# Expert weights through three landing places and on-chip moves, instead of straight into a ring of six buffers

## The reference, cut to what matters

```python
def block_step(out, inp):
    toks, gw, e = inp
    xb = t[toks]
    a = jnp.minimum(xb @ w_gate[e] + b_gate[e], SWIGLU_LIMIT)
    b = jnp.clip(xb @ w_up[e] + b_up[e], -SWIGLU_LIMIT, SWIGLU_LIMIT)
    hid = a * jax.nn.sigmoid(SWIGLU_ALPHA * a) * (b + 1)
    y = hid @ w_down[e] + b_down[e]
    return out.at[toks].add((y * gw[:, None]).astype(out.dtype)), None
```

## Time and profile before

| | us |
|---|---|
| median of 3 runs (1394.22 to 1398.82) | 1398.72 |
| span of the profiled execution, first to last instruction | 1396.9 |
| PE busy | 1252.0 |
| DVE busy | 402.7 |
| POOL busy | 121.0 |

### The profile page before, as it was taken

One profiled execution on the slowest core, in us unless ns is written; L12 is line 12 of the kernel. 1 busy time (PEld: TensorE's weight loads), 2 busy tenths in 40 slices (PEclk: granted clock), 3 DMA queues, 4 the chain that ended last, 5 costly groups with the idle time before them and its releaser, 6 DMA issues.

```text
span 1396.9 us, 24933 instructions
## 1 busy us (share of the span) xinstructions
PE 1252.0 (90%) x10197; PEld 555.7 (40%) x10198; DVE 402.7 (29%) x896; ACT 260.1 (19%) x501; POOL 121.0 (9%) x168
## 2 busy tenths in 40 slices
PE   5999898568989999988999889988989999999996
PEld 2445445466654333333333333333333333333432
DVE  1265469817855121111111111111111112111112
ACT  2421432336041111111111111100000101100102
POOL 0211540185000000000000000000000000000000
PEclk9999999769988999999999999999999999999998
DMA  9958010010476999999999999999999699969994
GB/s 354 397 182 316 31 61 30 5 34 31 180 308 254 426 426 428 427 428 427 426 426 426 426 428 427 427 427 425 426 426 420 268 427 426 426 266 426 428 427 179
DMA packets 48135, 458.59 MB, mean 328 GB/s; under 512 B 4417, under 2 KB 4817, under 8 KB 22737
## 3 DMA queue, kind: packets, MB, share of 16 engines
q1 hardware_dynamic: 48080, 457.81, 79.1%
HBM read 456.15 MB, written 1.05 MB: 327 GB/s over the span
## 4 chain that ended last, share of the span: by engine, by line
PE 54%; DMA 34%; DVE 7%; issue 2%; ACT 1%; POOL 1%; DVEq 0%; SPq 0%; POOLq 0%; ACTq 0%
DMA arena<-in_w_up 33%; PE bank L1163 21%; PE bank L1190 8%; PE bank L673 7%; PE bank L1055 2%; PE bank L1124 2%; PE bank L584 2%; PE bank L544 1%; DVE arena L1737 1%; PE bank L1172 1%; DVE arena L2266 1%; DVE arena L2263 1%; DVE arena L2261 1%; DMA arena<-in_x 1%; PE bank L904 1%
## 5 line engine op out<-in xcount | busy, mean ns | idle before, releaser
L1163 PE MATMUL bank<-arena 128*64 128x512 f32 x2176 | 484.6, 595 | 43.7 <-DMA arena<-in_w_up 22.5
L1163 PEld LDWEIGHTS bank<-arena 128*64 128x64 f32 x2176 | 150.1, 136 | 359.3 <-issue 263.9
L1190 PE MATMUL bank<-arena 128*64 128x512 f32 x1088 | 239.2, 592 | 0.0
L2259 DVE TENSOR_SCALAR arena<-bank 128x512 f32<-128x512 f32 x34 | 23.6, 693 | 403.3 <-PE bank L1163 403.3
L1190 PEld LDWEIGHTS bank<-arena 128*64 128x64 f32 x1088 | 75.9, 136 | 140.5 <-issue 138.0
L673 PE MATMUL bank<-arena 128*128 128x512 f32 (+1 forms) x320 | 123.7, 540 | 0.0
L673 PEld LDWEIGHTS bank<-arena 128*128 128x128 f32 x320 | 60.7, 195 | 58.2 <-issue 55.3
L2190 DVE TENSOR_SCALAR arena<-arena 96x64 bf16<-96x64 f32 x35 | 8.8, 251 | 224.6 <-PE bank L1190 224.6
L1133 PE MATMUL bank<-arena 64*128 64x512 f32 x280 | 69.6, 614 | 0.8 <-ACT arena L1552 0.8
L1124 PE MATMUL bank<-arena 128*128 128x64 bf16 x1680 | 62.8, 198 | 1.1 <-DVE arena L2186 1.1
L1124 PEld LDWEIGHTS bank<-arena 128*128 128x128 bf16 x1680 | 62.9, 118 | 1.2 <-DVE arena L2186 1.2
(11 more groups left out here) (352 smaller groups left out, 1029.2 us busy)
## 6 DMA issues: line engine op xcount, KB each, us to landing
arena<-in_w_gate SPq DMA_DIRECT2D x64, 2048.0 KB, 22.5
arena<-in_w_up SPq DMA_DIRECT2D x64, 2048.0 KB, 24.1
arena<-in_w_down SPq DMA_DIRECT2D x64, 2048.0 KB, 22.0
arena<-in_w_ada SPq DMA_DIRECT2D x12, 2048.0 KB, 9.7
arena<-in_wfm SPq DMA_DIRECT2D x20, 512.0 KB, 3.4
arena<-in_wz SPq DMA_DIRECT2D x4, 1024.0 KB, 14.3
arena<-in_w_out SPq DMA_DIRECT2D x2, 2048.0 KB, 8.3
arena<-in_x SPq DMA_DIRECT2D x2, 1024.0 KB, 7.6
```

Source lines behind the costliest of these rows:

```text
L1163: last = mm(ps[m][64 * c_:64 * c_ + 64, :], xcT[:, k, :], ring[:, 2 * h_ + m, k % 4, 512 * c_:512 * c_ + 512], start=False, stop=(k == KT ...
L1190: last = mm(ps[2][64 * c_:64 * c_ + 64, :], hidT[:, k % 4, 64 * (k // 4):64 * (k // 4) + 64], ring[:, 4 + h_, k % 4, 512 * c_:512 * c_ + 5 ...
L2259: v.tensor_scalar(hid[:, 0], ps[0][:, :], LIMIT, None, ALU.min).then_inc(*L.mark("a"))
```

## The change

Three further buffers of 128 x 4096, `places` (`ahead0` to `ahead2`), stand beside the ring. For every expert after the first, a piece n no longer lands in the ring but in place n % 3, and an engine moves it on to its buffer in the ring: POOL pieces 0 to 3 (`move_up`, four copies of 128 x 1024 for each piece), DVE pieces 4 and 5 (one `tensor_scalar` of 128 x 4096 each, times 1.0, after `hid` in each turn). In a further block of the same expert, and in turn 1, DVE's copy reads and writes the same buffer (`same`, `stays`), so that nothing is changed.

POOL moves piece n of expert i when it has landed and PE has marked piece n in the last block of expert i-1. PE waits for the moves instead of the transfers, except in turn 1. SP issues, for expert i in this order: piece 0 after POOL has moved piece 3 of expert i-1; pieces 1 and 2 after DVE has moved pieces 4 and 5 in the first block of expert i-1; pieces 3, 4 and 5 after POOL has moved pieces 0, 1 and 2 of expert i.

The first expert's pieces still go straight into the ring, piece 0 without the wait for `mixT`, 1 and 2 after two steps of DVE (`Oss`, `gdn`). Pieces 0, 1 and 2 of expert 1 are issued ahead of the loop: 0 after `mixT` and `Yss`, 1 and 2 after the router's products. To make room, the layout is changed: `hid`, `passed`, `wr` and the bias parts move into constants no longer used, `xcT`, `hidT`, `y`, `GT`, `Sg` and `Sb` into `gates`, `acc` and the output rows (`final`) into the ring, and `wout`, `yt` and `mixT` to the ring's pieces 3 to 5. DVE loads two more values from memory to registers in each turn. The core of the diff:

```diff
+AHEAD = 3
+CHUNK_W = 1024
...
+    e = put(keep, ("mix", 2 * D), ("h", 2 * D), ("hT", KT * 256), ("route", 1500), ("bias", 3 * 512), ("hp", 3 * D))
+    at["ahead2"] = (at["rows"][0] + 2 * D, 4096)
+    at["ahead1"] = (at["h"][0], 4096)
+    e = put(e, ("ahead0", 4096), ("ring", PIECES * 4096))
+    assert at["ahead2"][0] + 4096 == at["h"][0] and at["ahead1"][0] + 4096 == at["route"][0]
+
+    put(at["ring"][0] + 3 * 4096, ("wout", KT * D), ("yt", 4 * 512), ("mixT", KT * 256))
+    assert at["wout"][0] >= at["O"][0] + 1024 and at["yt"][0] >= at["kdS"][0] + 8192
...
-        acc = view(area("acc"), 2, D)
+        acc = view(area("ring", 0, 2 * D), 2, D)
+        final = view(area("ring", 4096, 2 * D), 2, D)
...
+        places = [area(f"ahead{i}") for i in range(AHEAD)]
...
+            def piece_ahead(n, expert):
+
+                m, c = order[n]
+                src = halves[m][bass.ds(expert, 1), c].rearrange("e p n -> p (e n)")
+                sp.dma_start(places[n % AHEAD], src).then_inc(sems(f"in_ring{n}"), 16)
+
+            piece(0, 0)
+            sp.wait_ge(*L.at("dve", "Oss", 1))
+            piece(1, 0)
+            sp.wait_ge(*L.at("dve", "gdn", 1))
+            piece(2, 0)
             sp.wait_ge(*L.at("pe", "mixT", 0, 1))
-            for n in range(3):
-                piece(n, 0)
+            sp.wait_ge(*L.at("dve", "Yss", 1))
+            piece_ahead(0, 1)
...
             piece(5, 0)
+            sp.wait_ge(*L.at("pe", "logit", 1))
+            sp.wait_ge(*L.at("act", "hparts", 0, 1))
+            sp.wait_ge(*L.at("dve", "rest", 0))
+            sp.wait_ge(*L.at("pool", "rest", 1))
+            piece_ahead(1, 1)
+            sp.wait_ge(*L.at("dve", "h", 1))
+            sp.wait_ge(*L.at("dve", "hparts", 1))
...
-            def pieces(blocks, expert):
-                L.begin_turn(blocks)
-                for n in range(PIECES):
-                    sp.wait_ge(*L.at("pe", "piece", n))
-                    piece(n, expert)
-
+            def later_half(expert):
+
+                for n in range(AHEAD, PIECES):
+                    sp.wait_ge(*L.at("pool", "copy", n - AHEAD, turn=expert))
+                    piece_ahead(n, expert)
+
+            def next_half(blocks, expert):
+
+                sp.wait_ge(*L.at("pool", "copy", 3, turn=expert, back=1))
+                piece_ahead(0, expert)
+                for n in range(1, AHEAD):
+                    sp.wait_ge(*L.at("dve", "copy", n + AHEAD, turn=blocks, back=-1))
+                    piece_ahead(n, expert)
+
+            later_half(1)
             sp.wait_ge(*L.at("dve", "table"))
-            with sp.Fori(1, E_N) as i:
-                pieces(sp.value_load(intab[0:1, bass.ds(i + (BLOCKS - 1), 1)], min_val=1, max_val=BLOCKS - 1), i)
+            with sp.Fori(2, E_N) as i:
+                next_half(sp.value_load(intab[0:1, bass.ds(i + (BLOCKS - 2), 1)], min_val=1, max_val=BLOCKS - 2), i)
+                later_half(i)
...
+            def landed(n, expert, first):
+
+                return (sems(f"in_ring{n}"), 16) if first else L.at("pool", "copy", n, turn=expert)
...
-                        pe.wait_ge(sems(f"in_ring{2 * h_ + m}"), expert * 16 + 16)
+                        pe.wait_ge(*landed(2 * h_ + m, expert, first))
...
-                    pe.wait_ge(sems(f"in_ring{4 + h_}"), expert * 16 + 16)
+                    pe.wait_ge(*L.at("dve", "copy", 4 + h_))
...
+            v.memset(same[0:1, 0:1], 1).then_inc(*L.mark())
+            v.tensor_tensor(same[0:1, 1:BLOCKS], table[0:1, 1:BLOCKS], table[0:1, 0:BLOCKS - 1], ALU.is_equal).then_inc(*L.mark())
...
+                own_expert = dve.value_load(intab[0:1, bass.ds(turn - 1, 1)], min_val=0, max_val=E_N - 1)
+                stays = dve.value_load(same[0:1, bass.ds(turn - 1, 1)], min_val=0, max_val=1)
...
+                for n in range(4, PIECES):
+                    from_, to = AT[f"ahead{n % AHEAD}"][0], AT["ring"][0] + 4096 * n
+                    dve.wait_ge(sems(f"in_ring{n}"), own_expert * 16 + 16)
+                    dve.wait_ge(*L.at("pe", "piece", n, back=1))
+                    v.tensor_scalar(arena[:, to:to + 4096], arena[:, bass.ds(stays * (to - from_) + from_, 4096)], 1.0, None, ALU.mult).then_inc(*L.mark("copy", n))
...
+            L.stage("moe")
+            pool.sem_inc(*L.open_loop())
+
+            def move_up(blocks, expert):
+
+                for n in range(4):
+                    pool.wait_ge(sems(f"in_ring{n}"), expert * 16 + 16)
+                    pool.wait_ge(*L.at("pe", "piece", n, turn=blocks))
+                    pool.sem_inc(sems("pool_go"), 1)
+                    for lo in range(0, 4096, CHUNK_W):
+                        g_.tensor_copy(area("ring", 4096 * n + lo, CHUNK_W), places[n % AHEAD][:, lo:lo + CHUNK_W]).then_inc(*L.mark("copy", n))
+
+            pool.wait_ge(*L.at("dve", "table"))
+            with pool.Fori(1, E_N) as i:
+                L.begin_turn(i)
+                move_up(pool.value_load(intab[0:1, bass.ds(i + (BLOCKS - 1), 1)], min_val=1, max_val=BLOCKS - 1), i)
+                L.end_turn()
```

More of the change, by code:

```diff
@@ L110, in own, with at @@
         return self.sem, self.n if self.turn is None else self.turn * self.per + self.n
-    def at(self, who, *step, back=0):
+    def at(self, who, *step, back=0, turn=None):
         name, value = self.book.old.get((who,) + step) or self.book.new.get((who,) + step) or (f"{who}_dry", 1)
@@ L151, in put @@
         return base
-    keep = put(0, ("const", NCONST), ("x", 2 * D), ("rows", 4 * D), ("cols", 8 + 20 * 5 + 8),
-               ("small", 720), ("gates", 2304))
+    keep = put(0, ("const", NCONST), ("x", 2 * D), ("cols", 8 + 20 * 5 + 8),
+               ("small", 720), ("gates", 2304), ("rows", 4 * D))
     ops = put(keep, ("kT", 4 * 512), ("qT", 4 * 256), ("bT", 2 * 512), ("cT", 2 * 256), ("k_tm", 4 * 512),
@@ L175, in lay_out_sbuf @@
     put(at["Xn"][0], ("O", 1024))
[L176 to L184, removed]
+    e = put(keep, ("mix", 2 * D), ("h", 2 * D), ("hT", KT * 256), ("route", 1500), ("bias", 3 * 512), ("hp", 3 * D))
[5 more added lines that the diff above has]
+    assert at["wout"][0] >= at["O"][0] + 1024 and at["yt"][0] >= at["kdS"][0] + 8192
+    e = put(CONSTS["tri"][0], ("bst", D), ("b_part01", D), ("wr", 256))
+    put(at["wr"][0], ("same", BLOCKS))
+    assert e <= CONSTS["before"][0]
+    put(CONSTS["tri"][0], ("hid", 4 * 512))
+    put(CONSTS["tri"][0], ("passed", BLOCKS * 32))
+    put(at["cols"][0], ("b_part2", 512))
+    put(at["cols"][0], ("hid4", 512))
+    e = put(at["gates"][0] + 128, ("xcT", 512), ("hidT", 512), ("y", 512), ("GT", 256), ("Sg", 256), ("Sb", 64))
+    assert e <= at["gates"][0] + at["gates"][1]
     return at
@@ L221, in layer_program @@
         xin = view(area("x"), 2, D)
-        rows = view(area("rows"), 4, D)
+        rows = [area("rows", D * at_, D) for at_ in (2, 3, 1, 0)]
         npm = area("cols", 0, 8)
@@ L336, in layer_program @@
         bias = area("bias").bitcast(BF16).rearrange("p (m d) -> p m d", m=3)
-        acc = view(area("acc"), 2, D)
+        acc = view(area("ring", 0, 2 * D), 2, D)
+        final = view(area("ring", 4096, 2 * D), 2, D)
         xcT = view(area("xcT"), KT, SLOT)
-        hid = view(area("hid"), 6, 512)
+        hid = [area("hid", 512 * i, 512) for i in range(4)] + [area("hid4")]
         hidT = view(area("hidT"), 4, 128)
@@ L379, in layer_program @@
         gsel = route(2, 1)
-        passed = view(area("rows", 0, BLOCKS * 32), BLOCKS, 32)
+        passed = view(area("passed"), BLOCKS, 32)
         selb = route(32).bitcast(BF16)
+        same = area("same").bitcast(I32)
         def norm_of(i):
@@ L445, in _ @@
                 load(f"win{i}", area("win", i * 1024, 1024), wfm[i])
-            load("wrow", area("rows", 0, 3 * D), wrow)
+            load("wrow", area("rows", 2 * D, 2 * D), wrow[:, 0:2 * D])
+            load("wrow", rows[2], wrow[:, 2 * D:3 * D])
             def load_brow(which):
@@ L1065, in _ @@
                     at_ = 2 * (KT * j + k)
-                    last = mm(ps[4][:, at_:at_ + 2], rows[:, row, 128 * k:128 * k + 128], ident[:, 0:2], start=True, stop=True)
+                    last = mm(ps[4][:, at_:at_ + 2], rows[row][:, 128 * k:128 * k + 128], ident[:, 0:2], start=True, stop=True)
             last.then_inc(*L.mark("rcols"))
@@ L1171, in block_of_rows @@
                 for k in range(4):
-                    last = nc.tensor.transpose(unit(ps[0], k), hid[:, 4, k:512:4], ident)
+                    last = nc.tensor.transpose(unit(ps[0], k), hid[4][:, k:512:4], ident)
                 last.then_inc(*L.mark("hidT"))
@@ L1751, in row_out @@
                     dve.wait_ge(*L.own())
-                    v.scalar_tensor_tensor(out=rows[:, row, r], in0=b_, scalar=1.0 if which == 2 else 0.0, in1=rows[:, row, r],
+                    v.scalar_tensor_tensor(out=rows[row][:, r], in0=b_, scalar=1.0 if which == 2 else 0.0, in1=rows[row][:, r],
```

38 lines of the change are left out of this document (20 added, 18 removed).

## The result

The changed kernel takes **1455.26 us** (median of 4 runs, 1454.26 to 1456.55) against 1398.77 in the same comparison: ratio **1.040, 95% interval 1.037 to 1.044**. The profiled execution's span is 1452.5 us. In its code the moves are L2580 (POOL) and L2325 (DVE), PE's gate and up L1212, bias L1205, SP's issue L516, DVE's chain behind piece 3 L2315, L2317, L2320.

The account below looks back on a forecast made before the run. Transfers, 3.25 us per expert slower than PE, were taken to bound the kernel. 7 x 26.2 + 27 x 30.5 + 6.6 = 1013.6, from 427.7 plus 15.0 tail, 3 contention and 1.8 gave 1461 us; range 1428 to 1512.

Parts of the forecast that it names:

- The loop: From DVE's copy of piece 4 to the next turn's: transfers, POOL's copy, PE, DVE; 30.5 us per one-block expert.
- rival 1: The loop hides under the transfers, period 29.47 us, 1433 us in all; chance 0.22.
- No lead: In the loop no lead in weights builds up, so 27 turns take 30.5 us.
- The seven turns at 26.2: Turns 1, 2, 19, 24, 25, 30, 31, their pieces released a turn before, run at PE's 26.2 us.
- 3 x 2 x 0.5 = 3 us: In turns 1, 24, 30 two DVE operations each wait half a 1.03 us POOL chunk; 3 us added.
- Turn 1 begins where it does: Nothing before 427.7 us waits for a weight, so the prologue leaves turn 1's start unchanged; priced at nothing.
- Turns 1 and 2 have their weights: Pieces 0 to 2 of expert 1 are landed when turn 1 begins, so both turns take 26.2 us.
- The sum: Turns and pause 1013.6 us, from 427.7 plus 15.0 tail: span 1456; contention 3 gives 1459; median 1461.
- SP waits mostly on DVE's copy line: Sign for the forecast: SP's waits mostly on DVE's copy, once per expert, and POOL's lines for the rest.
- The rule of the port: GpSimd and certain VectorE operations take a shared port pair exclusively; whole-instruction blocking would put 14 us nearer than 3.
- the 14 that I had worked out as the worst: Worst contention of DVE with POOL's copies: 2 us in each of seven turns, 14 us.
- The price of a piece: POOL's copy of one piece: 4.1 us taken; the skill's estimated 3.5 gave period 29.9, span some 1440.

Follow-up runs that it names:

- run 1: Changed kernel with DVE's copy of piece 4 placed ahead of its clamp behind piece 3: 1429.69 us, 1.024 times the kernel before the change.
- run 2: Changed kernel with one more DVE operation between `hid` and the copies, making them 0.76 us later: 1477.86 us, 1.056 times the kernel before.
- run 5: Changed kernel with POOL moving all six pieces, DVE none, and SP waiting on POOL alone: 1403.85 us, 1.005 times the kernel before.
- run 11: Changed kernel with only the two multiplications behind piece 3 reading one operand from PSUM: 1453.73 us, 1.039 times the kernel before.
- run 6: As run 5, with POOL's copies in chunks of 512 columns instead of 1024: 1414.20 us, 1.012 times the kernel before.
- run 8: As run 5, with the clamp of up and the first product written back into their PSUM bank: 1389.81 us, 0.993 times the kernel before.
- run 4: Changed kernel with POOL moving each piece in one copy of 4096 columns instead of four of 1024: 1461.98 us, 1.046 times the kernel before.
- run 9: As run 8, with each piece moved in one copy of 4096 columns: 1399.60 us, 0.999 times the kernel before.

## Why the prediction was right, point by point

- **The loop.** All its terms are in the ordinary turn above: three transfers 17.8 (17.9 forecast), POOL 3.99 (4.1), PE 3.65 (3.68), DVE 2.1 (2.14) and its copy 2.25 (2.35). The 0.3 for the hops between engines came from no row; the gaps in this turn sum to 0.2. Each term was a little smaller, so 29.9 to 30.0 for 30.5. Runs 1 and 2 show that this path sets the turn: shortened, the turn falls to 29.4 and no further; lengthened by 0.76, it grows by 0.62. Run 1 is rival 1 made real, at 1429.7 where 1433 was worked out.
- **No lead.** Right: 26 turns at about 30. Run 1 keeps the loop under the transfers and still loses 32 us; run 5, in which the issue of the next expert's pieces no longer hangs on `hid`, is within 7 us of before. So of the 56.5 us, some 26 are the loop: about 14 in the ordinary turns, and as much in turns 3, 20, 26 and 32, which run near PE's pace once it is short. About 21 are the rest of the lead, and what is left is mostly DVE and POOL in each other's way (turns 1, 24 and 30). An issue a whole turn ahead of use is what the old rule had.
- **The seven turns at 26.2.** Only turns 2, 25 and 31 took 26.2 or 26.3. Turns 24 and 30 took 2.9 and 1.9 more, and run 11 takes 2.6 and 1.7 of that away. The step "3 x 2 x 0.5 = 3 us" had the mechanism and too small a size: L2317 and L2320 took 1.50 and 1.40 in both turns, so PE stood 1.5 us longer in each, not 1.0. Behind the stop in turn 24 the granted clock was 0.59 from 1136 to 1140, which cost 1.3 more; behind the same stop in turn 30 it stayed at 1.00. Turn 19 took 28.4, 2.2 more; it took 27.7 in the kernel before too, so most of that I had overlooked.
- **Turn 1.** "Turn 1 begins where it does" was off by 4.3 us, to the good, and that was luck: versions 2 and 11, with the same prologue, began turn 1 at 431.5 and 432.3, and all experiments lie between 423.8 and 432.3. "Turns 1 and 2 have their weights" was right and not enough: turn 1 took 31.6, 5.4 more. Of this, PE's longer stop behind DVE is 2.6, since the table of blocks and the preparations on DVE fell under POOL's copies; the clock of 0.50 behind that stop is 1.1, and the clock of 0.50 at the start of the turn, ahead of any copy, is 1.6. The contention was looked for only in the two operations behind piece 3; run 11, which frees these, leaves turn 1 long. In turns 1, 24 and 30 together contention held PE for 5.6 us, where 3 were forecast, and the low clock behind two of the stops cost 2.4, which the forecast had at nothing.
- **The sum** came out as near as it did by luck, since errors offset each other: about 0.5 us less in the ordinary turns (-12), the seven turns more than forecast (+9.5), turn 1 sooner (-4), so a span of 1452.5 for 1459.
- **The signs.** "SP waits mostly on DVE's copy line" did not come out: POOL's line has 546.5 us in 120 waits, DVE's 327.8 in 60, though the longest, 24.9, is DVE's. How long SP waits for whom does not say which of them sets the turn; runs 1 and 2 do. The 30 us between turns (30.5 forecast) and POOL's busy time (511 us more for 508) came out.
- **The rule of the port.** The Trainium skill, "SBUF — State Buffer", section "SBUF: two separate sides", has the loser blocked for the whole instruction. Most rows agree: 0.69 us becomes up to 1.5 behind copies of 1 us, and 3.49 for 48 columns behind copies of 3.6. Run 6 does not: 7.55 us behind copies of 0.56 is a wait for many instructions, and there the measurement decides. The two multiplications with one input from PSUM aren't held at all (0.70 and 0.69 us, run 8). The cost lay between my 3 us and the 14 that I had worked out as the worst.
- **The price of a piece.** The Trainium skill, "GPSIMD Engine Reference", section 3.1, gives an estimated 3.5 us for a piece: 3.61 in one copy, 3.99 in four.

## What to carry to other kernels

Before a transfer is hung on a new releaser, ask how long before its use that releaser comes; three more buffers gave nothing in the changed kernel because the refill waited for the end of a chain that the same refill feeds. The sum around such a loop is the turn, and busy shares (DVE 42%, POOL 44%) don't show it. When GpSimd is given copies, look at every operation of VectorE on SBUF that runs meanwhile, small ones too. A long copy holds them longer (runs 4 and 9), but a row of very short ones without a gap held one for 7.55 us (run 6). Taking one operand of the critical operations from PSUM freed them (run 8). And look at TensorE's granted clock behind each stop: the stop can cost again.

## What the runs showed of the hardware that was not expected

- A wait of VectorE for GpSimd can last over many of GpSimd's instructions: 7.55 us for an operation of 0.69, against copies of 0.56 (run 6, turns 24 and 30).
- A move can cost the mover too. Where DVE's copies met POOL's (timeline of the changed kernel), POOL took 7.49 us for 3.99 and DVE 5.33 for 4.49:

```profile
987.08 5.33 DVE L2325 TENSOR_SCALAR arena<-arena 128x4096 f32 x2
```

```profile
987.78 7.49 POOL L2580 COPY arena<-arena 128x1024 f32<-128x1024 f32 x4 [11.58 <-DMA arena<-in_w_gate]
```

- Two more values loaded from memory to registers per turn raise DVE's idle time ahead of the first preparation from 42.8 us before to 91.0 (L2302 of the page after) in 34 turns: 0.7 us for each. It costs nothing in ordinary turns, where DVE then waits 10.65 us for PE (ahead of L2313 in the turn above). The line before:

```profile
L2248 DVE TENSOR_SCALAR arena<-arena 128x128 f32<-128x128 f32 x68 | 20.6, 346 | 42.8 <-issue 28.4 <-DVE arena L2190 14.4
```

- The chain that the page prints went through POOL and piece 0. It looks the same in run 1, whose turn is shorter. In it, piece 3's transfer counts from its issue to its landing, with the wait behind pieces 1 and 2 in the queue, and these are the ones that DVE's copies release: in the ordinary turn 510.63 to 521.80, 11.2 us for a transfer that takes 4.9 of the stream. Only moving DVE's copy, ahead in run 1 and back in run 2, showed the loop.
